# Exponentials read from PSUM with the maximum as bias, in the attention stage of a hybrid encoder step

## The reference

```python
s = jnp.einsum('bnqkgd,bnskd->bnkgqs', q, k) * (B_HEAD_DIM ** -0.5)
s = jnp.where(mask[None, :, None, None], s, -jnp.inf)
m = jnp.maximum(jnp.max(s, axis=-1, keepdims=True), sink)
p = jnp.exp(s - m)
p = p / (jnp.sum(p, axis=-1, keepdims=True) + jnp.exp(sink - m))
return jnp.einsum('bnkgqs,bnskd->bnqkgd', p, v)
```

## Time and profile before

| | |
|---|---|
| median of 3 runs | 1034.31 us (1033.92 to 1034.66) |
| the profiled execution, its own time | 1033.92 us |
| its span, first to last instruction | 1032.1 us |
| busy: PE, VectorE, ScalarE, GpSimd | 1011.6, 640.2, 516.0, 48.4 us |
| mean granted clock of PE, as a share of full speed | 1.000 |
| the attention stage in the span | about 88.4 to 134.7 us |

### The profile page before, as it was taken

The page is one execution under the profiler, slowest core; times in us unless marked ns, Lnnn a source line. Parts: engine busy times, 40 slices in busy tenths (PEclk is TensorE's granted clock), DMA queues, the critical chain, the costliest instruction groups (busy, mean ns, idle before and its releaser), DMA issues.

```text
span 1032.1 us, 19073 instructions
## 1 busy us (share of the span) xinstructions
PE 1011.6 (98%) x7907; PEld 992.5 (96%) x7907; DVE 640.2 (62%) x956; ACT 516.0 (50%) x859; POOL 48.4 (5%) x55
## 2 busy tenths in 40 slices
PE   8999899999999999999999999999999999999997
PEld 6898799899999999999999999999999999999997
DVE  5397754887555555544569877798755555444643
ACT  6632465655444444444456655676544444444552
POOL 0081210000000000000000000002000000000000
PEclk9999999999999999999999999999999999999999
DMA  8322122566666555546655575556655555455554
GB/s 280 82 83 70 42 81 63 164 188 180 184 185 176 170 165 164 164 126 184 189 156 154 154 215 171 163 160 188 192 168 167 167 166 147 143 167 168 155 162 150
DMA packets 307431, 161.28 MB, mean 156 GB/s; under 512 B 14667, under 2 KB 304307, under 8 KB 307345
## 3 DMA queue, kind: packets, MB, share of 16 engines
q1 hardware_dynamic: 306880, 159.61, 53.1%
q0 software_dynamic: 224, 0.35, 0.1%
q10 hardware_dynamic: 240, 0.10, 0.0%
HBM read 157.46 MB, written 2.58 MB: 155 GB/s over the span
## 4 chain that ended last, share of the span: by engine, by line
PE 87%; DVE 8%; ACT 2%; issue 1%; DMA 1%; ACTq 0%; POOL 0%; DVEq 0%
PE ps L554 28%; PE ps L556 28%; PE ps L555 27%; DVE wlo L1496 2%; DVE tmp L1780 1%; ACT whi L1069 1%; PE ps L803 1%; PE ps L817 1%; DVE xlo L1789 1%; PE ps L638 0%; DVE s_sb L1662 0%; DMA gain_rows<-in_c_scale_dram 0%; DVE den L1672 0%; DVE top L1656 0%; DMA raw<-in_ffn_w_in_dram 0%
## 5 line engine op out<-in xcount | busy, mean ns | idle before, releaser
L1496 DVE TENSOR_TENSOR wlo<-raw,whi 128x1024 fp32r<-128x1024 f32 (+2 forms) x332 | 368.6, 1111 | 259.4 <-ACT whi L1069 259.1
L554 PE MATMUL ps<-xhi,whi 128*128 128x256 f32 (+1 forms) x1600 | 466.9, 292 | 4.7 <-DVE xlo L1789 2.7
L556 PE MATMUL ps<-xhi,wlo 128*128 128x256 f32 (+1 forms) x1600 | 460.8, 288 | 0.0
L555 PE MATMUL ps<-xlo,whi 128*128 128x256 f32 (+1 forms) x1600 | 459.8, 287 | 0.0
L1069 ACT ACTIVATE whi<-raw 128x1024 fp32r<-128x1024 f32 (+2 forms) x332 | 315.8, 954 | 221.1 <-PE ps L556 199.3
L554 PEld LDWEIGHTS ps<-xhi,whi 128*128 128x128 f32 x1600 | 300.9, 188 | 8.2 <-DVE xlo L1789 3.6
L555 PEld LDWEIGHTS ps<-xlo,whi 128*128 128x128 f32 x1600 | 301.0, 188 | 0.0
L556 PEld LDWEIGHTS ps<-xhi,wlo 128*128 128x128 f32 x1600 | 300.9, 188 | 0.0
L554 PE MATMUL ps<-mhi_b,whi 128*128 128x288 f32 x352 | 104.7, 297 | 0.0
L556 PE MATMUL ps<-mhi_b,wlo 128*128 128x288 f32 x352 | 104.3, 296 | 0.0
L555 PE MATMUL ps<-mlo_b,whi 128*128 128x288 f32 x352 | 102.7, 292 | 0.0
(11 more groups left out here) (223 smaller groups left out, 902.1 us busy)
## 6 DMA issues: line engine op xcount, KB each, us to landing
raw<-in_ffn_w_in_dram SPq DMA_DIRECT2D x176, 512.0 KB, 3.9
raw<-in_ffn_w_out_dram SPq DMA_DIRECT2D x64, 384.0 KB, 3.2
raw<-in_ffn_w_out_dram SPq DMA_DIRECT2D x64, 320.0 KB, 2.9
raw<-in_ab_w_in_dram SPq DMA_DIRECT2D x10, 512.0 KB, 4.5
raw<-in_ab_w_out_dram SPq DMA_DIRECT2D x10, 256.0 KB, 2.9
raw<-in_ab_w_out_dram SPq DMA_DIRECT2D x20, 128.0 KB, 3.1
x_tok<-in_x_prompt_dram SPq DMA_DIRECT2D x4, 512.0 KB, 6.8
raw<-in_ab_w_in_dram SPq DMA_DIRECT2D x8, 256.0 KB, 3.9
```

The source lines that it names most:

```text
L554: pe.matmul(out, wh, xh, start=first, stop=False)
L555: pe.matmul(out, wh, xl, start=False, stop=False)
L556: return pe.matmul(out, wl, xh, start=False, stop=last)
L1496: dve.tensor_tensor(wlo[:, s, 0:n], raw[:, m % NRAW, 0:n], whi[:, s, 0:n].bitcast(F32), ALU.subtract)\
```

## The change

The maximum is no longer subtracted by VectorE. `peak` now holds its negative (minimum of `-scale * top` and the negated sink), and ScalarE uses it as the bias of the exponential, reading the scores from PSUM with the scale, one instruction for each block of 128 columns since the bias is one value per partition. Each of these instructions also delivers the row sum to `den2`, by a read of the accumulator that follows it in the instruction stream. The two instructions for the shifted scores and the sum of the exponentials leave VectorE's program. For the sample the masked scores still go through SBUF.

The bank of chunk `c-2` is now free when its exponentials are done, so `scores(c)` waits for `exp_done` in place of `shifted`. ScalarE waits, ahead of chunk `c`'s exponentials, for chunk `c-2`'s transposes and reciprocals, whose buffers it writes.

VectorE's order changes: low part 13 moves from ahead of the loop to behind chunk 0's maxima; low parts 14, 15 and 16 move one iteration on, to behind the next chunk's maxima (the last one stands where no chunk follows); the copies of u stand between a chunk's maxima and its denominator; the first half copy goes ahead of the loop. The u steps of PE are dealt out anew.

```diff
--- before.py
+++ after.py
@@ -59,9 +59,9 @@
 
 
 U_FIRST = 4
-U_STEPS = (2, 2, 2, 3, 2, 2, 2, 3, 2, 4, 4)
+U_STEPS = (2, 3, 3, 2, 2, 2, 2, 3, 2, 4, 3)
 U_THROUGH = (2, 5, 8)
-U_HALF_THROUGH = (1, 4, 7)
+U_HALF_THROUGH = (3, 7)
 
 GATE_BANKS = (0, 2, 4, 6)
 
@@ -394,7 +394,7 @@
         rope_done, k_s_ready, k_turned, k_out_ready = sem("rope_done"), sem("k_s_ready"), sem("k_turned"), sem("k_out_ready")
         gate_done, gate_biased, sinks_ready = sem("gate_done"), sem("gate_biased"), sem("sinks_ready")
         scored, s_masked, topped, peaked = sem("scored"), sem("s_masked"), sem("topped"), sem("peaked")
-        shifted, sink_shifted, exp_done, summed = sem("shifted"), sem("sink_shifted"), sem("exp_done"), sem("summed")
+        sink_shifted, exp_done = sem("sink_shifted"), sem("exp_done")
         den_ready, rden_ready, p_ready = sem("den_ready"), sem("rden_ready"), sem("p_ready")
         p_turned, p_t_ready, pv_done, att_hi, att_lo = sem("p_turned"), sem("p_t_ready"), sem("pv_done"), sem("att_hi"), sem("att_lo")
         u_evacuated, u_half_out, u_half_done, u_gelu, ya_ready, ya_hi, ya_lo = sem("u_evacuated"), sem("u_half_out"), sem("u_half_done"), sem("u_gelu"), sem("ya_ready"), sem("ya_hi"), sem("ya_lo")
@@ -693,7 +693,7 @@
                 if c == 1:
                     pe.wait_ge(gate_biased, 3)
                 if c >= 2:
-                    pe.wait_ge(shifted, NKV * (c - 1))
+                    pe.wait_ge(exp_done, c - 1)
                 if c == NCH:
                     pe.wait_ge(k_s_ready, 1)
                     pe.wait_ge(kc_ready, 1)
@@ -1177,11 +1177,21 @@
 
             def exps(c):
                 w = CHUNK if c == 0 else P
-                n = 2 if c == NCH else 4
-                s = s_sb[:, c % 2, 0:n * P].rearrange("p (c s) -> p c s", c=n)[:, :, 0:w]
+                n, b = (2, c % 2) if c == NCH else (4, c % 2)
+                npg = n // NKV
                 act.wait_ge(sink_shifted, c + 1)
-                act.activation(den[:, c % 2, 0:n], sunk[:, c % 2, 0:n], ACT.Exp)
-                act.activation(s, s, ACT.Exp).then_inc(exp_done, 1)
+                if c >= 2:
+
+                    act.wait_ge(p_turned, c - 1)
+                    act.wait_ge(rden_ready, c - 1)
+                act.activation(den[:, b, 0:n], sunk[:, b, 0:n], ACT.Exp)
+                for j in range(n):
+                    g, k = divmod(j, npg)
+                    p = s_sb[:, b, j * P:j * P + w]
+                    src, scale = (p, 1.0) if c == NCH else (flat(2 + 2 * b + g, k * P, w), SCALE)
+                    op = act.activation(p, src, ACT.Exp, scale=scale, bias=peak[:, b, j:j + 1],
+                                        accum_out=den2[:, b, j:j + 1])
+                op.then_inc(exp_done, 1)
 
             def keep_turned(c):
                 act.wait_ge(p_turned, c + 1)
@@ -1539,10 +1549,10 @@
             lo_part(4)
 
             dve.wait_ge(sinks_loaded, 16)
-            dve.tensor_copy(sink_p[0:CHUNK, :], sinks[0:CHUNK, 0:NQ:2])
-            dve.tensor_copy(sink_p[CHUNK:P, :], sinks[CHUNK:P, 1:NQ:2])
+            dve.tensor_scalar(sink_p[0:CHUNK, :], sinks[0:CHUNK, 0:NQ:2], -1.0, None, ALU.mult)
+            dve.tensor_scalar(sink_p[CHUNK:P, :], sinks[CHUNK:P, 1:NQ:2], -1.0, None, ALU.mult)
             for a in range(4):
-                op = dve.tensor_copy(sink_s[a * DEC:(a + 1) * DEC, :], sinks[a * DEC:(a + 1) * DEC, a:NQ:4])
+                op = dve.tensor_scalar(sink_s[a * DEC:(a + 1) * DEC, :], sinks[a * DEC:(a + 1) * DEC, a:NQ:4], -1.0, None, ALU.mult)
             op.then_inc(sinks_ready, 1)
             lo_part(5)
             lo_part(6)
@@ -1628,7 +1638,6 @@
                     bias_gate(1)
             bias_gate(2)
             bias_gate(3)
-            lo_part(13)
 
 
             def shift(c):
@@ -1642,11 +1651,9 @@
                         for g in range(NKV)]
                 scale = SCALE
                 dve.wait_ge(scored, c + 1)
-                if c >= 2:
+                if c == NCH:
 
                     dve.wait_ge(p_turned, c - 1)
-                if c == NCH:
-
                     for g in range(NKV):
                         dve.scalar_tensor_tensor(dst[:, g, :], srcs[g][:, 0, :], SCALE, mask_s[:, :],
                                                  ALU.mult, ALU.add).then_inc(s_masked, 1)
@@ -1655,22 +1662,13 @@
                 for g in range(NKV):
                     dve.tensor_reduce(top[:, b, g * npg:(g + 1) * npg], srcs[g], AX.X, ALU.max).then_inc(topped, 1)
                 dve.wait_ge(topped, NKV * (c + 1))
-                dve.scalar_tensor_tensor(peak[:, b, 0:n], top[:, b, 0:n], scale, sink, ALU.mult, ALU.max).then_inc(peaked, 1)
+                dve.scalar_tensor_tensor(peak[:, b, 0:n], top[:, b, 0:n], -scale, sink, ALU.mult, ALU.min).then_inc(peaked, 1)
                 dve.wait_ge(peaked, c + 1)
-                for g in range(NKV):
-                    part = slice(g * npg, (g + 1) * npg)
-                    dve.scalar_tensor_tensor(dst[:, part, :], srcs[g], scale,
-                                             peak[:, b, part].unsqueeze(2).broadcast_to([P, npg, w]),
-                                             ALU.mult, ALU.subtract).then_inc(shifted, 1)
-                dve.tensor_tensor(sunk[:, b, 0:n], sink, peak[:, b, 0:n], ALU.subtract).then_inc(sink_shifted, 1)
+                dve.tensor_tensor(sunk[:, b, 0:n], peak[:, b, 0:n], sink, ALU.subtract).then_inc(sink_shifted, 1)
 
             def denominator(c):
                 n, b = (2, c % 2) if c == NCH else (4, c % 2)
-                w = CHUNK if c == 0 else P
-                p = s_sb[:, b, 0:n * P].rearrange("p (c s) -> p c s", c=n)[:, :, 0:w]
                 dve.wait_ge(exp_done, c + 1)
-                dve.tensor_reduce(den2[:, b, 0:n], p, AX.X, ALU.add).then_inc(summed, 1)
-                dve.wait_ge(summed, c + 1)
                 dve.tensor_tensor(den2[:, b, 0:n], den2[:, b, 0:n], den[:, b, 0:n], ALU.add).then_inc(den_ready, 1)
                 dve.wait_ge(den_ready, c + 1)
                 dve.reciprocal(rden[:, b, 0:n], den2[:, b, 0:n]).then_inc(rden_ready, 1)
@@ -1693,18 +1691,22 @@
 
             dve.wait_ge(sinks_ready, 1)
             dve.wait_ge(set_sample, 1)
+            evacuate_u_half(0)
             for i in range(NCH + 3):
                 if i <= NCH:
                     shift(i)
-                    denominator(i)
+                if i == 0:
+                    lo_part(13)
+                if i - 1 in U_THROUGH:
+                    lo_part(14 + U_THROUGH.index(i - 1))
                 if i in U_HALF_THROUGH:
-                    evacuate_u_half(U_HALF_THROUGH.index(i))
+                    evacuate_u_half(U_HALF_THROUGH.index(i) + 1)
                 if i in U_THROUGH:
                     evacuate_u(U_THROUGH.index(i))
+                if i <= NCH:
+                    denominator(i)
                 if i >= 2:
                     attended_lo(i - 2)
-                if i in U_THROUGH:
-                    lo_part(14 + U_THROUGH.index(i))
             evacuate_u_half(3)
             evacuate_u(3)
```

## The result

| | before | changed |
|---|---|---|
| median of 5 runs, us | 1034.51 (1033.92 to 1037.02) | 1029.58 (1029.15 to 1029.63) |
| ratio, 95% interval | | 0.9944 [0.9933, 0.9955] |
| profiled execution, us (its span) | 1033.92 (1032.1) | 1029.58 (1027.7) |

The changed kernel is faster, by 4.9 us between the medians; by the ratio it is 0.56%, with 0.45 to 0.67% as its interval. The direction is the one forecast. The size is not: 1030.4 us was forecast, and the lower end of the range, 1029.6, is missed by 0.02 us. The error is small against the time but a fifth of the effect, so what has to be found is which terms of the sum were wrong.

The account below looks back on a forecast made before the run. PE was taken as the bound, its 4.52 us of waits all there is to win. -4.52 + 0.45 + 0.2 = -3.9 us from 1033.92 gives 1030.0, plus 0.39 to the median 1030.4 us; range 1029.6 to 1032.8, its own 1029.7 to 1031.4.

Parts of the forecast that it names:

- Item 1: VectorE, each chunk: shifted scores (0.67 us) and sum of exponentials (0.73 us) leave the chunk's string.
- Item 2: ScalarE, each chunk: one exponential of 0.61 us becomes four with accumulator reads, 1.6 us in all.
- q: ScalarE: time of one 128-column exponential with its accumulator read; taken as 0.40 us, between 0.39 and 0.51.
- Item 3: VectorE between maxima and denominator: weight low parts and u copies hidden beside ScalarE's exponentials, costed at nothing.
- Item 4: Chunk string: VectorE's output low part waits 0.4 us for ScalarE; 4.1 us from maxima to maxima.
- Item 5: PE: one more u step in chunk 1 and in chunk 2, one fewer at the end; two steps last 1.49 us.
- +0.45 us: PE before the sample's product: a new wait of 0.45 us, as one u step fewer stands ahead of it.
- -4.52 us: PE, chunk 0's scores to the last u projection step: all 4.52 us of reported idle time goes.
- for hand-offs that appear once larger waits are gone I add 0.2: Attention stage: allowance of 0.2 us for small hand-offs that show once larger waits are gone.
- (a): ScalarE's accumulator reads cost more, q 0.45 to 0.55; chunk string bounds the stage, 1032.5 us at 0.51; chance 0.22.
- (c): End of stage: low part 16 late or PE's waits wrongly named, 1033.5 to 1034.3 us; chance 0.08.
- (b): ScalarE: each exponential and read drains fully, 0.64 us each; slower by 2.3 us, 1036.6 us; chance 0.08.

Follow-up runs that it names:

- e7: Changed kernel with the exponentials' row sums (accumulator reads) left out: median 1029.75 us, ratio 0.9938.
- e4: Changed kernel with one u step moved from iteration 9 to iteration 10: median 1029.29 us, ratio 0.9936.
- e3: Changed kernel with two extra tiny ScalarE instructions behind each of a chunk's first three exponentials: median 1032.63 us, ratio 0.9967.
- e5: Changed kernel with four extra tiny ScalarE instructions behind each of a chunk's first three exponentials: median 1037.36 us, ratio 1.0010.
- e1: Kernel before with the change's order of work and u steps, its softmax untouched: median 1031.31 us, ratio 0.9956.
- e8: Changed kernel with the four weight low parts put back at their old places: median 1034.03 us, ratio 0.9977.
- e9: Changed kernel with the old distribution of u steps: median 1028.96 us, ratio 0.9931.
- e2: Kernel before with the new softmax, in the old order and with the old u steps: median 1033.13 us, ratio 0.9981.
- e12: Kernel before with only its first half copy of u moved ahead of the loop: median 1034.91 us, ratio 0.9990.
- e10: Changed kernel run again, unaltered: median 1029.47 us, ratio 0.9936.
- e11: Kernel before run again, unaltered, for a second profile: median 1036.59 us, ratio 0.9997.

## Why the prediction was right and wrong

**The bound: right.** PE sets the stage and idles for probabilities and u copies. e7 (exponentials quicker, no gain) and e4 (no idle time, stage 47.53) show it.

**Item 1, what VectorE loses: right.** The rows of VectorE in chunk 3 have maxima, peak and sunk, then the moved work; 10.8 us less on the page.

**Item 2, q: too high, and it mattered.** 0.344 us, where 0.40 was taken and 0.39 held for the best case. The exponential starts its read after 0.25, not 0.28, and the read its successor after 0.09, not 0.11: both pieces were put together from rows of other instructions, and each was a little too long. The string by the prediction's own formula, 2.5 + 4q, is 3.88 us; 3.91 was measured. e3 and e5 fit it as well (4.46 and 5.00). A q of 0.40 would have cost time: 4q is then 0.22 us longer, and over chunks 3 to 7 that puts chunk 7's probabilities 1.1 us behind PE; e3's 3.12 us for 0.56 us of 4q give 1.25. (Both are estimates; no run has this q.)

**Item 3, low parts and copies at nothing: right.** It was also the larger part of the change, which the working, busy with q, did not say: 3.87 of 5.26 us by e1, where u copies and steps move too, and again by e8 for the low parts alone. The prediction's remark that with exponentials as short as before about 1 us of each low part would be bare is what e1's rows show.

**Item 4, the low part of the output waits for ScalarE: right**, 0.39 us per chunk in the rows above. Twice it is over 1 us (1.13 at 100.91 and 1.15 at 127.31), which the prediction had named as a sign of being wrong; the first held nothing up, and the second is the low part that the sample's product waits 0.34 us for.

**Item 5 and "+0.45 us": right**, 0.34 measured.

**The sum: the failed step is "-4.52 us", under the reading "these waits are all there is to win".** It took the idle time that the profile reports for the cost of the waits, and the waits cost 5.6 us. Idle time is counted from the end of the last matmul, and in the rows of the changed kernel a matmul of 256 columns is 0.28 to 0.29 us long while its successor starts after 0.12 (98.00 and 98.13). Where PE waits, the last one is shown to its full length, so 0.16 to 0.17 us of the wait are not reported as idle. Starts alone show the size, without any modelled end. e9 gives PE the same instructions in the same order as the kernel before, and PE has no waits there. Set side by side, the kernel before falls back by 0.74, 1.15, 0.84, 0.42, 1.61 and 0.65 us at its six waits (0.58, 1.07, 0.67, 0.25, 1.46 and 0.49 reported) and by some 0.2 more in the starts between them, 5.6 us in all. The other runs agree. The first part less its reported idle time is 39.4 to 39.7 us with six waits (the kernel before, e2, e8, e12), 39.11 with three (e1), 38.50 with one (the change) and 38.45 with none (e4, e9). So the six waits of the kernel before cost 1.1 us beyond what the profile gives as idle. It is also the main part of the 1.4 us by which PE seemed less busy.

That PE could collect all of it needed the second mis-sized term. The prediction had string and PE arrive together at chunk 7's transposes, 121.8 and 121.9. Measured on the time axis of the kernel before (less the 0.56 us of later start) PE was there at 120.8, 1.1 us earlier, and the string, at q = 0.344, at 120.8 too. With q = 0.40 as taken it would have come at about 121.9, PE would have waited, and the stage would have gained about 4.1 us, near the 3.9 of the sum (an estimate). The first error alone would hardly have shown; the smaller q brought it out. With the measured sizes the sum is -4.52 - 1.1 + 0.34 = -5.3 us; the stage gave -5.26. A smaller failed step is "for hand-offs that appear once larger waits are gone I add 0.2": none appeared.

In the stage the sum was 1.4 us short. In the time it shows as 0.8, because the later start and the 0.3 us behind the stage gave 0.86 back in this pair of profiles, while the added 0.39 us from the profiled execution to the median did not apply to the changed kernel (1029.58 both). That the result lies only 0.02 us outside the range is therefore chance. The range failed at its lower end because it was made of q from 0.39 to 0.44 only: it had bounds for the cost of the new work, and none for the worth of the old waits. By the prediction's own working a smaller q could not even reach 1029.7, since PE's own work bounds below 0.40, and -4.52 + 0.45 gives 1030.2.

**The rivals.** (a) and (c) did not occur: q is below (a)'s range, and low part 16 delayed nothing. (a)'s price was about right: at q = 0.48 the prediction's string gives a wait of 100.8 + 4 x 4.42 + 4.92 - 121.9 = 1.5 us, so a stage of 53.16 - 3.9 + 1.5 = 50.8; e3 took 51.02. (b)'s length of string makes the stage longer than before from a q between 0.48 (e3) and 0.62 (e5). The Trainium skill ("VectorE: DVE Perf Modes", section on the TRN2 errata) advises tiles of 512 elements or more because a fixed cost is exposed between small ones. It says so of operations that read SBUF, and these exponentials read PSUM. A cost of that kind is there all the same: four without reads of the accumulator take 4 x 0.25 = 1.00 us (e7) and with them 1.38, for what one exponential of 512 columns did in 0.52. It fell on an engine that had just the time, and e7 shows that even 0.4 us less of it would have brought nothing.

What stays open: why the medians differ by more than the stage. It was 4.9 us in the first comparison and 7.0 in e10's, for the same 5.26 us of stage. In the table every run from e1 on with a stage, except e11, has a median that is 1.2 to 2.3 us lower against that kernel than its stage says, also e2 with six waits and e5 with eight. So the kernel before has in its median some 1.7 us that its first profile does not show and that waits of PE alone do not bring. One fall of the clock as in e11's profile (1.43 us) is as large, and so is a later start (1.49 us); only single executions were profiled, and which of them it is was not shown.
